# A decoder layer's opening: keys projected by token tile, the norm scale moved into the weights, bias rows built later

## The chip, the cores and the metric

One core of one Trainium2 chip. The metric is the device time of one execution in microseconds (us); less is better. The kernel before took a median of 1637.75 us in 3 runs (1637.44 to 1637.79).

## The reference, cut to what matters

```python
h = rmsnorm(x, norm_g)                       # x: 1024 tokens x 2048, float32
proj = einsum('bsd,de->bse', h, w_in)        # 5456 columns
xa, ga, q, ckv, gb, qi, ki, wi = split(proj) # ki: 64 index keys, wi: 16 head weights, ckv: 256 latent
ya = rglru(xa) * silu(ga)
yb = sparse_attention(q, rmsnorm(ckv), qi, layernorm(ki), wi, bias from rel_bias) * silu(gb)
x = x + concat(ya, yb) @ w_out
return rmsnorm(x, final_norm_g)
```

`rmsnorm(x, g)` is `x * rsqrt(mean(x*x)) * g`. The factor `g` belongs to a column of x, which is a row of `w_in`, so it can be multiplied into either.

## The kernel before, in words

Everything is float32, and each product is made of three: an operand is cut into a high part (rounded to the format that TensorE multiplies quickly) and the low rest, and `triple` adds low x high, high x low and high x high.

**Input.** x comes in 8 tiles of 128 tokens, 1 MB each (`xin`, four buffers). For a tile ScalarE (ACT) sums the squares (`square`, L704) and takes the root (`root_x`, L709). VectorE (DVE) inverts it and multiplies the tile by it and by `g_bc`, the norm scale on all partitions (`norm_x`, L1344). TensorE (PE) transposes the tile with 16 instructions (`turn_x`, L1034), ACT copies the high part out of PSUM (`high_x`, L715) and DVE makes the low part (`low_x`, L1351). The results, `hT_hi` and `hT_lo`, stay for the whole projection.

**Projection.** `w_in` is taken in 43 tiles of 128 columns (the first, `T_KW`, has the 80 columns of keys and head weights). A tile comes in four pieces, with one buffer each. SyncE (SP) issues the load when the piece's low part of the last tile is made. ACT copies the high part (`high`, L724) once PE has used the last tile's piece (`w_used`), and GpSimd (POOL) subtracts it from the raw weights (`low`, L643). PE (`project_tile`, L1023 to L1025) runs 6 matmuls of 512 columns for each of the 16 rows of blocks.

**Order on PE at the start.** The bias matmul (L1015), whose result ACT copies, 8 partitions wide, and SP stores 128 times to DRAM as `bias_rows` (1.5 MB, L459). Then the transposes. With tiles 4 to 7 goes a quarter each of the keys of the first 512 tokens; the second 512 follow. Then tile 1 (`T_C`), the means of the keys (L1070), tile 2, the variance (L1076), tile 3, the latent's mean square (L1088), and tile 4 with the index scores in it (`score`, L1110).

**Orders by hand.** Each engine runs its list in program order. On SP each load of weights stands behind the waits of all before it, and the loads of tile 1 behind the bias store. On ACT, after the keys' layer norm, stand all four pieces of `high(4)`, then an exponential with its table (L776), the latent's root (L778), and the copies of tile 3's result (`stacks`, L788 and L789), which DVE completes (L1409, L1410). The first score waits for these. Later stages (LRU from tile 11, attention projection from tile 27) run through the same `high` and `low`.

Of the kernel before, what the change touches and what calls it, by code (L numbers as in the profile page):

```python
# [117 lines left out]
def layer(nc, a, out):  # L118
# [11 lines left out]
    with ctx:  # L130
# [22 lines left out]
        w_nat = sb("w_nat", [P, QB, IH])  # L153
        sums = sb("sums", [P, QB, 3])
# [533 lines left out]
        def _(act):  # L688
# [23 lines left out]
            def high_x(i):  # L712
                for j in range(2):
                    act.wait_ge(x_tp, 2 * i + j + 1)
                    nc.scalar.activation(  # L715
                        hT_hi[:, 8 * j:8 * j + 8, i * P:(i + 1) * P],
                        x_bank(i, j).rearrange("p (t s) -> p t s", s=P), ACT.Copy).then_inc(h_hi, 1)

            def high(t, js=range(PIECES), n=P):

                for j in js:
                    act.wait_ge(w_in_s[j], 16 * t + 16)
                    act.wait_ge(w_used, 4 * t + j + 1)
                    nc.scalar.activation(w_hi[:, j, :, 0:n], w_raw[:, j, :, 0:n], ACT.Copy).then_inc(w_hi_s, 1)  # L724
# [281 lines left out]
        def _(pe):  # L1006
            nc.tensor.sem_inc(w_used, PIECES)
# [663 lines left out]
```

## Time and profile before

| | us |
|---|---|
| median of 3 runs | 1637.75 |
| the profiled execution | 1639.89 |
| its span, first to last instruction | 1638.2 |
| PE busy | 1585.0 |
| DVE busy | 855.5 |
| ACT busy | 581.0 |
| POOL busy | 424.3 |

Times on the profile's clock start at the first instruction. Matmul ends are modelled, so consecutive matmuls overlap in the rows: their pace is read from start to start. PEld is the load of a matmul's weights, which runs beside the matmul ahead of it. "Idle before" names the work that the profile holds responsible for the end of the wait.

### The profile page before, as it was taken

The numbers are of one execution on the slowest core, as the hardware profiler recorded it, in microseconds if no ns is written. First come the engines' busy times: TensorE is split into PE (matmuls) and PEld (weight loads), VectorE is DVE, ScalarE is ACT, GpSimd is POOL, SyncE is SP. The second block draws the span as 40 slices with busy tenths as digits, with TensorE's granted clock in tenths as the row PEclk, the third lists the DMA queues.
The fourth block names the chain that finished last, engine by engine and source line by source line (L and its number), as shares of the span: only waits on it lengthen the run. The fifth ranks groups of instructions, "written<-read, shape, count | busy, mean of one in ns | idle before, by whom it ended". The sixth has DMA issues, their size and how long they took to land.

```text
span 1638.2 us, 21182 instructions
## 1 busy us (share of the span) xinstructions
PE 1585.0 (97%) x7403; PEld 1314.9 (80%) x7403; DVE 855.5 (52%) x1497; ACT 581.0 (35%) x849; POOL 424.3 (26%) x285
## 2 busy tenths in 40 slices
PE   4999999999999999999999999999998899999998
PEld 3678999988888888888888888777776788888886
DVE  7417555577777877875555555277777100031003
ACT  7225555434444343332111111355555222232320
POOL 1112222222222222222222222110010344444650
PEclk8999999999999999999999999999999999999999
DMA  7411211112221122223222221321222523237322
GB/s 260 86 46 45 66 44 40 37 48 62 61 61 44 49 67 67 67 84 96 76 72 77 70 77 51 110 84 62 64 80 74 222 91 102 90 97 301 131 88 103
DMA packets 132302, 141.35 MB, mean 86 GB/s; under 512 B 8511, under 2 KB 103841, under 8 KB 129953
## 3 DMA queue, kind: packets, MB, share of 16 engines
q1 hardware_dynamic: 130720, 136.55, 26.8%
q0 software_dynamic: 1536, 4.20, 0.8%
q8 instruction: 28, 0.46, 0.1%
q14 instruction: 18, 0.14, 0.0%
HBM read 116.08 MB, written 24.64 MB: 86 GB/s over the span
## 4 chain that ended last, share of the span: by engine, by line
PE 83%; issue 8%; DVE 4%; ACT 2%; DMA 1%; DVEq 0%; POOL 0%; SPq 0%; ACTq 0%; POOLq 0%
PE ps L1023 17%; PE ps L1024 17%; PE ps L1025 17%; PE ps L1283 6%; PE ps L1285 6%; PE ps L1284 6%; PE ps L1224 2%; PE ps L1110 2%; PE ps L1112 2%; PE ps L1188 2%; PE ps L1201 1%; PE ps L1310 1%; PE ps L1309 1%; PE ps L1308 1%; PE ps L1208 1%
## 5 line engine op out<-in xcount | busy, mean ns | idle before, releaser
L1023 PE MATMUL ps<-hT_hi,w_lo 128*128 128x512 f32 (+2 forms) x1376 | 524.8, 381 | 2.5 <-POOL w_lo L643 2.5
L1024 PE MATMUL ps<-hT_lo,w_hi 128*128 128x512 f32 (+2 forms) x1376 | 522.8, 380 | 0.0
L1025 PE MATMUL ps<-hT_hi,w_hi 128*128 128x512 f32 (+2 forms) x1376 | 522.6, 380 | 0.0
L643 POOL TENSOR_TENSOR w_lo<-w_raw,w_hi 128x512 fp32r<-128x512 f32 (+1 forms) x172 | 240.5, 1402 | 780.9 <-ACT w_hi L724 780.9
L1023 PEld LDWEIGHTS ps<-hT_hi,w_lo 128*128 128x128 f32 (+1 forms) x1376 | 257.7, 187 | 49.9 <-issue 4.0
L1024 PEld LDWEIGHTS ps<-hT_lo,w_hi 128*128 128x128 f32 (+1 forms) x1376 | 257.5, 187 | 45.9 <-issue 0.4
L1025 PEld LDWEIGHTS ps<-hT_hi,w_hi 128*128 128x128 f32 (+1 forms) x1376 | 257.5, 187 | 45.6 <-issue 0.2
L724 ACT ACTIVATE w_hi<-w_raw 128x512 fp32r<-128x512 f32 (+1 forms) x172 | 106.6, 628 | 504.7 <-PE ps L1025 483.4
L1283 PE MATMUL ps<-wo_hi,hT_lo 128*128 128x512 f32 x448 | 175.2, 391 | 3.1 <-DVE hT_lo L1551 3.1
L1610 DVE TENSOR_TENSOR res<-ps,res 128x512 f32<-128x512 f32 x32 | 21.9, 691 | 295.8 <-PE ps L1285 244.9
L1284 PE MATMUL ps<-wo_lo,hT_hi 128*128 128x512 f32 x448 | 174.9, 390 | 0.0
L1285 PE MATMUL ps<-wo_hi,hT_hi 128*128 128x512 f32 x448 | 174.8, 390 | 0.0
L1459 DVE MATCH_REPLACE8 scores<-top,scores 128x384 f32<-128x384 f32 (+2 forms) x192 | 165.8, 876 | 0.0
L1454 DVE MAX8 top<-scores 128x8 f32<-128x384 f32 (+2 forms) x192 | 155.3, 879 | 0.9 <-DVE sg L1491 0.2
L679 POOL TENSOR_TENSOR wo_lo<-wo_raw,wo_hi 128x1024 fp32r<-128x1024 f32 x48 | 116.1, 2419 | 148.4 <-ACT wo_hi L956 148.4
L1434 DVE SCALAR_TENSOR_TENSOR scores<-relu,w_nat,scores 128x384 f32<-128x384 f32 (+2 forms) x96 | 94.7, 997 | 79.1 <-ACT relu L798 79.0
L956 ACT ACTIVATE wo_hi<-wo_raw 128x1024 fp32r<-128x1024 f32 x48 | 50.8, 1061 | 191.4 <-PE ps L1285 191.4
L798 ACT ACTIVATE relu<-ps 128x384 f32<-128x384 f32 (+2 forms) x96 | 72.9, 760 | 80.0 <-PE ps L1112 63.6
L1283 PEld LDWEIGHTS ps<-wo_hi,hT_lo 128*128 128x128 f32 x448 | 84.5, 189 | 20.7 <-issue 3.3
L1284 PEld LDWEIGHTS ps<-wo_lo,hT_hi 128*128 128x128 f32 x448 | 84.5, 189 | 17.7
L1285 PEld LDWEIGHTS ps<-wo_hi,hT_hi 128*128 128x128 f32 x448 | 84.5, 189 | 17.7
L1498 DVE TENSOR_TENSOR rg<-ps,ig 128x1024 f32<-128x1024 f32 x8 | 9.8, 1225 | 158.2 <-ACT ig L876 140.3
(179 smaller groups left out, 1716.8 us busy)
## 6 DMA issues: line engine op xcount, KB each, us to landing
w_raw<-in_w_in SPq DMA_DIRECT2D x168, 256.0 KB, 2.9
wo_raw<-in_w_out SPq DMA_DIRECT2D x64, 512.0 KB, 3.6
xin<-in_x SPq DMA_DIRECT2D x8, 1024.0 KB, 5.3
res<-in_x SPq DMA_DIRECT2D x8, 1024.0 KB, 9.4
out<-res SPq DMA_DIRECT2D x16, 512.0 KB, 4.0
y_lru_dram<-sg SPq DMA_DIRECT2D x8, 512.0 KB, 2.8
q_dram<-av SPq DMA_DIRECT2D x8, 512.0 KB, 3.8
gate_dram<-rg SPq DMA_DIRECT2D x8, 512.0 KB, 4.4
```

The source lines that it names most:

```text
L643: nc.gpsimd.tensor_tensor(w_lo[:, j, :, 0:n], w_raw[:, j, :, 0:n], w_hi[:, j, :, 0:n].bitcast(F32), ALU.subtract).then_inc(w_lo_s, 1)
L679: nc.gpsimd.tensor_tensor(wo_lo[:, j % 2, :, :], wo_raw[:, j % 4, :, :], wo_hi[:, j % 2, :, :].bitcast(F32), ALU.subtract).then_inc(wo_lo_ ...
L724: nc.scalar.activation(w_hi[:, j, :, 0:n], w_raw[:, j, :, 0:n], ACT.Copy).then_inc(w_hi_s, 1)
L1023: nc.tensor.matmul(o, wlo, hi, start=(kt == 0), stop=False)
L1024: nc.tensor.matmul(o, whi, lo, start=False, stop=False)
L1025: return nc.tensor.matmul(o, whi, hi, start=False, stop=(kt == KT - 1))
L1283: nc.tensor.matmul(o, hT_lo[:, kt, tok], wo_hi[:, j % 2, k, :], start=(kt == 0), stop=False)
L1284: nc.tensor.matmul(o, hT_hi[:, kt, tok], wo_lo[:, j % 2, k, :], start=False, stop=False)
L1285: last = nc.tensor.matmul(o, hT_hi[:, kt, tok], wo_hi[:, j % 2, k, :], start=False, stop=(kt == KT - 1))
L1434: stt(acc, relu[m % 2][:, 0:w], w_nat[:, q, ds(head, 1)], acc, ALU.mult, ALU.add).then_inc(ix_acc, 1)
L1454: found = step.did(nc.vector.max(top8[:, q, :], scores[:, off(q):off(q) + (q + 1) * P]))
L1459: marked = step.did(nc.vector.match_replace(left, top8[:, q, :], left, TAKEN))
```

## The change

- The scale `norm_g` comes as 16 rows, is turned into a column per block (`g_col`), and is no longer applied to x. DVE's pass over x is a `tensor_scalar`. POOL multiplies each raw weight piece by it in place, ahead of ACT's high part.
- Weights of keys are loaded behind the first two x tiles; POOL alone scales and cuts them. Each of the first four token tiles gets its keys at once, as 48 matmuls of 128 columns. With the last four goes a quarter each of tile 1 for the first 512 tokens. Keys of the second 512 and the second half of tile 1 follow.
- All transposes use the same two PSUM tiles `X`.
- The bias matmul comes after the keys, on 128 output partitions (each head 16 times). The store reads 128 partitions, and stands on SP behind the loads of tile 2. The wait for it moves to the latent's root.

```diff
--- before.py
+++ after.py
-        g_bc = s0("g_bc", [P, D])
+        kw_hi = s0("kw_hi", [P, KT, KW], F32R)
+        kw_lo = s0("kw_lo", [P, KT, KW], F32R)
...
-        bias_sb = s0("bias_sb", [NH, BR])
+        rel_wide = s0("rel_wide", [BUCKETS, NH, COPIES])
+        bias_sb = s0("bias_sb", [NH * COPIES, BR])
...
+            def x_next(i):
+                sp.wait_ge(x_tp, 2 * (i - XB) + 2)
+                sp.dma_start(xin[:, i % XB, :], x[i * P:(i + 1) * P, :]).then_inc(x_rest[i - XB], 16)
+            sp.dma_start(g_rows[:, :], a["norm_g"][0].rearrange("(k p) -> k p", p=P)).then_inc(g_in, 16)
             x_load(0)
-            sp.dma_start(g_bc[:, :], a["norm_g"].broadcast_to([P, D])).then_inc(g_in, 16)
             x_load(1)
+            weights(T_KW, COL_KI, KW)
+            for i in range(2, XB):
+                x_load(i)
+            x_next(XB)
+            x_next(XB + 1)
+            weights(T_C, COL_CKV)
+            x_next(XB + 2)
+            x_next(XB + 3)
             sp.dma_start(rel[:, :], a["rel_bias"]).then_inc(bias_in, 16)
             sp.dma_start(onehot[:, :], a["onehot"]).then_inc(bias_in, 16)
-            for i in range(2, XB):
-                x_load(i)
             sp.wait_ge(rows_clear, 1)
             rows = 0
             for name, n, m in [("conv_w", CONV * G, P), ("conv_b", G, P), ("lru_ba", G, P), ("lru_bx", G, P),
...
-            weights(T_KW, COL_KI, KW)
-            for i in range(QB - XB):
-                sp.wait_ge(x_tp, 2 * i + 2)
-                sp.dma_start(xin[:, i, :], x[(i + XB) * P:(i + XB + 1) * P, :]).then_inc(x_rest[i], 16)
+            weights(T_C + 1, COL_CKV + P)
             sp.wait_ge(bias_cp, 1)
-            sp.dma_start(bias_d.rearrange("h (p m) -> h p m", p=P),
-                         bias_sb[:, :].rearrange("h (o m) -> h o m", o=1).broadcast_to([NH, P, BR])).then_inc(bias_st, 16)
-            weights(T_C, COL_CKV)
-            weights(T_C + 1, COL_CKV + P)
+            sp.dma_start(bias_d.rearrange("h (c r m) -> (h c) r m", c=COPIES, m=BR),
+                         bias_sb[:, :].rearrange("h (o m) -> h o m", o=1).broadcast_to([P, P // COPIES, BR])
+                         ).then_inc(bias_st, 16)
             weights(T_QI, COL_QI)
             weights(T_QI + 1, COL_QI + P)
...
-            def low(t, n=P):
+            def gain(j, n):
+                return g_col[:, j * PK:(j + 1) * PK].rearrange("p (k o) -> p k o", o=1).broadcast_to([P, PK, n])
+            def scale_kw(j):
+                pool.wait_ge(w_in_s[j], 16)
+                part = w_raw[:, j, :, 0:KW]
+                nc.gpsimd.tensor_tensor(part, part, gain(j, KW), ALU.mult).then_inc(kw_g_s, 1)
+            def cut_kw(j):
+                part = slice(j * PK, (j + 1) * PK)
+                pool.wait_ge(kw_g_s, j + 1)
+                nc.gpsimd.tensor_copy(kw_hi[:, part, :], w_raw[:, j, :, 0:KW]).then_inc(w_hi_s, 1)
+                pool.wait_ge(w_hi_s, j + 1)
+                nc.gpsimd.tensor_tensor(kw_lo[:, part, :], w_raw[:, j, :, 0:KW], kw_hi[:, part, :].bitcast(F32),
+                                        ALU.subtract).then_inc(w_lo_s, 1)
+            pool.wait_ge(g_made, 1)
+            scale_kw(0)
+            for j in range(PIECES):
+                if j + 1 < PIECES:
+                    scale_kw(j + 1)
+                cut_kw(j)
+            def low(t):
                 for j in range(PIECES):
+                    part = w_raw[:, j, :, :]
+                    pool.wait_ge(w_in_s[j], 16 * t + 16)
+                    nc.gpsimd.tensor_tensor(part, part, gain(j, P), ALU.mult).then_inc(w_g_s, 1)
                     pool.wait_ge(w_hi_s, 4 * t + j + 1)
-                    nc.gpsimd.tensor_tensor(w_lo[:, j, :, 0:n], w_raw[:, j, :, 0:n],
-                                            w_hi[:, j, :, 0:n].bitcast(F32), ALU.subtract).then_inc(w_lo_s, 1)
-            low(T_KW, KW)
+                    nc.gpsimd.tensor_tensor(w_lo[:, j, :, :], part, w_hi[:, j, :, :].bitcast(F32), ALU.subtract
+                                            ).then_inc(w_lo_s, 1)
             with pool.Fori(1, TILES) as t:
                 low(t)
...
-                        x_bank(i, j).rearrange("p (t s) -> p t s", s=P), ACT.Copy).then_inc(h_hi, 1)
-            def high(t, js=range(PIECES), n=P):
+                        X[j][:, :].rearrange("p (t s) -> p t s", s=P), ACT.Copy).then_inc(h_hi, 1)
+            def high(t, js=range(PIECES)):
                 for j in js:
-                    act.wait_ge(w_in_s[j], 16 * t + 16)
+                    act.wait_ge(w_g_s, 4 * t + j - 3)
                     act.wait_ge(w_used, 4 * t + j + 1)
-                    nc.scalar.activation(w_hi[:, j, :, 0:n], w_raw[:, j, :, 0:n], ACT.Copy).then_inc(w_hi_s, 1)
+                    nc.scalar.activation(w_hi[:, j, :, :], w_raw[:, j, :, :], ACT.Copy).then_inc(w_hi_s, 1)
             act.wait_ge(eps_made, 1)
             square(0)
             root_x(0)
             square(1)
-            act.wait_ge(bias_mm, 1)
-            nc.scalar.activation(bias_sb[:, :], X[0][0:NH, 0:BR], ACT.Copy).then_inc(bias_cp, 1)
+            root_x(1)
             for i in range(QB):
-                if i + 1 < QB:
-                    root_x(i + 1)
+                high_x(i)
                 if i + 2 < QB:
                     square(i + 2)
-                high_x(i)
-                if i == XB - 2:
-                    high(0, n=KW)
-            high(1)
+                    root_x(i + 2)
+                if XB <= i:
+                    high(1, [i - XB])
             act.wait_ge(small_tp, 1)
             nc.scalar.activation(par_t[:, :], X[1][:, 0:PARS], ACT.Copy).then_inc(small_cp, 1)
-            act.wait_ge(bias_st, 16)
-            act.wait_ge(w_used, done(0))
+            act.wait_ge(bias_mm, 1)
+            nc.scalar.activation(bias_sb[:, :], X[0][:, 0:BR], ACT.Copy).then_inc(bias_cp, 1)
+            act.wait_ge(kw_used, 1)
             nc.scalar.activation(kw_sb[:, :], PJ[0][0:KW, :], ACT.Copy).then_inc(pj_free[0], 1)
             high(2)
...
             act.wait_ge(c_var, 1)
+            act.wait_ge(bias_st, 16)
...
-            pe.wait_ge(bias_in, 32)
-            nc.tensor.matmul(X[0][0:NH, 0:BR], rel[:, :], onehot[:, :], start=True, stop=True).then_inc(bias_mm, 1)
             pe.wait_ge(id_made, 1)
-            pe.wait_ge(bias_cp, 1)
-            def triple(o, j, k, tok, m):
+            pe.wait_ge(g_in, 16)
+            nc.tensor.transpose(X[0][:, 0:KT], g_rows[:, :], ident[0:KT, 0:KT]).then_inc(g_tp, 1)
+            pe.wait_ge(g_made, 1)
...
-                    pe.wait_ge(h_lo, 2 * i + j + (1 if i < XB else 3))
+                    if i > 0:
+                        pe.wait_ge(h_lo, 2 * i - 1 + j)
                     for n in range(8):
-                        last = nc.tensor.transpose(x_bank(i, j)[:, n * P:(n + 1) * P],
+                        last = nc.tensor.transpose(X[j][:, n * P:(n + 1) * P],
                                                    xin[:, i % XB, (8 * j + n) * P:(8 * j + n + 1) * P], ident[:, :])
                     last.then_inc(x_tp, 1)
-            for i in range(QB):
-                turn_x(i)
-                if i >= XB:
-                    pe.wait_ge(h_lo, 4 + 2 * XB)
-                    pe.wait_ge(w_lo_s, i - XB + 1 + PIECES)
-                    for k in range(PK):
-                        triple(PJ[0][0:KW, 0:NT], i - XB, k, slice(0, NT), KW)
-            pe.wait_ge(h_lo, 4 + 2 * QB)
-            def project_tile(t, par, turn, m=P, between=None, parts=ALL_TOKENS):
+            def keys_tokens(at, n):
+                for kt in range(KT):
+                    if kt % PK == 0:
+                        pe.wait_ge(w_lo_s, PIECES + kt // PK + 1)
+                    o, tok = PJ[0][0:KW, at:at + n], slice(at, at + n)
+                    nc.tensor.matmul(o, kw_lo[:, kt, :], hT_hi[:, kt, tok], start=(kt == 0), stop=False)
+                    nc.tensor.matmul(o, kw_hi[:, kt, :], hT_lo[:, kt, tok], start=False, stop=False)
+                    last = nc.tensor.matmul(o, kw_hi[:, kt, :], hT_hi[:, kt, tok], start=False, stop=(kt == KT - 1))
+                return last
+            def project_tile(t, par, turn, between=None, parts=ALL_TOKENS, js=range(PIECES), last_part=True):
                 pe.wait_ge(pj_free[par], turn + 1)
-                for j in range(PIECES):
+                for j in js:
                     pe.wait_ge(w_lo_s, 4 * t + j + 1 + PIECES)
                     for k in range(PK):
                         kt = j * PK + k
                         for at, tok, n in parts:
-                            last = triple(PJ[par][0:m, at:at + n], j, k, slice(tok, tok + n), m)
-                        if k == PK - 1:
+                            last = triple(PJ[par][:, at:at + n], j, k, slice(tok, tok + n))
+                        if k == PK - 1 and last_part:
                             last.then_inc(w_used, 1)
                         if between:
                             between(kt)
-            project_tile(0, 0, 0, m=KW, parts=ALL_TOKENS[1:])
+            turn_x(0)
+            for i in range(QB):
+                if i + 1 < QB:
+                    turn_x(i + 1)
+                if i < XB:
+                    pe.wait_ge(h_lo, 2 * i + 2)
+                    keys_tokens(i * P, P)
+                else:
+                    project_tile(T_C, 1, 0, parts=ALL_TOKENS[:1], js=[i - XB], last_part=False)
+            pe.wait_ge(h_lo, 2 * QB)
+            keys_tokens(NT, NT).then_inc(kw_used, 1)
             pe.wait_ge(small_in, 16 * 8)
             nc.tensor.transpose(X[1][:, 0:PARS], par_rows[:, :], ident[0:PARS, 0:PARS]).then_inc(small_tp, 1)
-            project_tile(1, 1, 0)
+            pe.wait_ge(rel_made, 1)
+            nc.tensor.matmul(X[0][:, 0:BR], rel_wide[:, :, :].rearrange("b h c -> b (h c)"), onehot[:, :],
+                             start=True, stop=True).then_inc(bias_mm, 1)
+            project_tile(T_C, 1, 0, parts=ALL_TOKENS[1:])
             pe.wait_ge(small_cp, 1)
             pe.wait_ge(pj_free[0], 2)
+            pe.wait_ge(bias_cp, 1)
...
-            dve.wait_ge(g_in, 16)
+            dve.wait_ge(g_tp, 1)
+            nc.vector.tensor_copy(g_col[:, :], X[0][:, 0:KT]).then_inc(g_made, 1)
             def norm_x(i):
                 dve.wait_ge(x_sd, i + 1)
                 root, inverse = (stat[:, k * XB + i % XB:k * XB + i % XB + 1] for k in (1, 2))
                 chain(nc.vector.reciprocal(inverse, root))
-                stt(xin[:, i % XB, :], xin[:, i % XB, :], inverse, g_bc[:, :], ALU.mult, ALU.mult
-                    ).then_inc(x_norm, 1)
+                nc.vector.tensor_scalar(xin[:, i % XB, :], xin[:, i % XB, :], inverse, None, ALU.mult
+                                        ).then_inc(x_norm, 1)
...
+            dve.wait_ge(bias_in, 32)
+            nc.vector.tensor_copy(rel_wide[:, :, :], rel[:, :].rearrange("b (h o) -> b h o", o=1).broadcast_to(
+                [BUCKETS, NH, COPIES])).then_inc(rel_made, 1)
             dve.wait_ge(x_tp, 2 * QB)
-            dve.wait_ge(bias_st, 16)
             chain(nc.vector.memset(ones_k[:, :], 1.0 / ID))
```

## Rows read from the trace of the kernel before

**Rows 1.** The page: busy time, share of the span and instructions of each engine

```profile
PE 1585.0 (97%) x7403; PEld 1314.9 (80%) x7403; DVE 855.5 (52%) x1497; ACT 581.0 (35%) x849; POOL 424.3 (26%) x285
```

**Rows 2.** Windows: length, busy us (instructions) by engine, granted clock, DMA share, GB/s

```profile
13.29:36.37 23.08, 13.62 (x81) 12.77 (x81) 21.94 (x18) 20.26 (x28) 3.40 (x4) 0.81 0.78 256
...
67.47:72.06 4.59, 4.59 (x13) 3.64 (x14) 4.55 (x7) 2.29 (x4) 3.64 (x3) 0.63 0.59 146
72.06:91.05 18.99, 18.99 (x84) 15.42 (x84) 0.54 (x4) 1.90 (x3) 3.89 (x3) 1.00 0.25 64
```

**Rows 3.** Timeline: start, us, engine, line (13.29: from the chain that ended last)

```profile
5.77 1.91 ACT L704 ACTIVATE junk<-xin 128x2048 bf16<-128x2048 f32 x1 [2.79 <-DMA xin<-in_x]
8.41 2.35 DVE L1344 SCALAR_TENSOR_TENSOR xin<-xin,stat,g_bc 128x2048 f32<-128x2048 f32 x1
10.80 1.91 ACT L704 ACTIVATE junk<-xin 128x2048 bf16<-128x2048 f32 x1 [2.69 <-DMA xin<-in_x]
...
13.29 3.66 PE ps L1034 x16
...
15.41 1.01 ACT L715 ACTIVATE hT_hi<-ps 128x1024 fp32r<-128x1024 f32 x1
16.45 1.23 DVE L1351 TENSOR_TENSOR hT_lo<-ps,hT_hi 128x1024 fp32r<-128x1024 f32 x1 [0.49 <-ACT hT_hi L715]
...
44.42 1.91 PE L1034 MATMUL ps<-ident,xin 128*128 128x128 f32 x16
```

**Rows 4.** Timeline from the bias store to the end of tile 1

```profile
29.62 0.87 SPq L459 DMA_DIRECT2D bias_rows<-bias_sb  x1
...
64.59 0.11 DVE L1363 MEMSET ones_k<- 64x64 f32 x1 [11.15 <-DMA bias_rows<-bias_sb]
...
67.47 0.47 PE L1023 MATMUL ps<-hT_hi,w_lo 128*128 128x512 f32 x1 [2.50 <-POOL w_lo L643]
...
91.05 0.64 PE L1070 MATMUL ps<-kw_sb,ones_k 64*64 64x512 f32 x1
```

**Rows 5.** Weight loads of two 128-column matmuls in a row, and mean by form

```profile
172.88 0.19 PEld L1112 LDWEIGHTS ps<-ki_hi,stack_a 128*128 128x128 f32 x1
172.99 0.19 PEld L1023 LDWEIGHTS ps<-hT_hi,w_lo 128*128 128x128 f32 x1
...
L1025 PEld LDWEIGHTS ps<-hT_hi,w_hi 128*128 128x128 f32 x1344 | 252.7, 188 | 42.8
L1025 PEld LDWEIGHTS ps<-hT_hi,w_hi 128*80 128x80 f32 x32 | 4.8, 151 | 2.8 <-issue 0.2
```

**Rows 6.** DVE and POOL groups by shape: count, busy us, mean ns

```profile
L1536 DVE TENSOR_SCALAR prob_sb<-prob_sb,sums 128x1024 f32<-128x1024 f32 x8 | 6.0, 753 | 0.3
L1536 DVE TENSOR_SCALAR prob_sb<-prob_sb,sums 128x896 f32<-128x896 f32 x8 | 5.5, 686 | 0.3
...
L643 POOL TENSOR_TENSOR w_lo<-w_raw,w_hi 128x320 fp32r<-128x320 f32 x4 | 3.4, 884 | 24.0 <-ACT w_hi L724 24.0
```

**Rows 7.** DMA from 17 to 18 us, while the keys' weights land

```profile
DMA packets 646, 0.20 MB, mean 200 GB/s; under 512 B 646, under 2 KB 646, under 8 KB 646
```

**Rows 8.** Timeline from the keys' layer norm to the first score

```profile
130.00 1.68 ACT L724 ACTIVATE w_hi<-w_raw 128x512 fp32r<-128x512 f32 x3
134.35 0.63 ACT L724 ACTIVATE w_hi<-w_raw 128x512 fp32r<-128x512 f32 x1 [2.68 <-PE ps L1025]
...
142.46 0.44 PE L1110 MATMUL ps<-ki_lo,stack_a 128*128 128x384 f32 x1 [0.61 <-DVE stack_b L1410]
```

**Rows 9.** L643 on POOL, 100 to 170 us: min/median/max ns; then its start at 130.71

```profile
L643 POOL TENSOR_TENSOR w_lo<-w_raw,w_hi x13: 1262/1296/2260, 99.5 to 169.7; 128x512 fp32r<-128x512 f32 x13
...
130.71 1.66 POOL L643 TENSOR_TENSOR w_lo<-w_raw,w_hi 128x512 fp32r<-128x512 f32 x1 [13.68 <-ACT w_hi L724]
```

**Rows 10.** Windows of tile 4 with its scores, and of one LRU group

```profile
142.46:165.00 22.54, 21.48 (x114) 19.77 (x115) 20.84 (x24) 10.34 (x16) 3.89 (x3) 1.00 0.14 49
466.00:512.24 46.24, 46.24 (x205) 38.29 (x205) 36.22 (x53) 18.44 (x22) 12.21 (x8) 1.00 0.21 60
```

More of the change, by code:

```diff
@@ L78 @@
 BR = 3 * P
+COPIES = P // NH
 OC = 512
@@ L153, in layer @@
         w_nat = sb("w_nat", [P, QB, IH])
+        g_col = sb("g_col", [P, KT])
         sums = sb("sums", [P, QB, 3])
@@ L166, in layer @@
         xin = s0("xin", [P, XB, D])
-        g_bc = s0("g_bc", [P, D])
+        kw_hi = s0("kw_hi", [P, KT, KW], F32R)
+        kw_lo = s0("kw_lo", [P, KT, KW], F32R)
         junk = s0("junk", [P, D], BF16)
         par_rows = s0("par_rows", [PARS, P])
+        g_rows = s0("g_rows", [KT, P])
         onehot = s0("onehot", [BUCKETS, BR])
         rel = s0("rel", [BUCKETS, NH])
-        bias_sb = s0("bias_sb", [NH, BR])
+        rel_wide = s0("rel_wide", [BUCKETS, NH, COPIES])
+        bias_sb = s0("bias_sb", [NH * COPIES, BR])
         p0.close()
@@ L303, in layer @@
         g_in = sem("g_in")
+        g_tp = sem("g_tp")
+        g_made = sem("g_made")
+        rel_made = sem("rel_made")
         x_in = [sem(f"x_in{i}") for i in range(XB)]
@@ L311, in layer @@
         w_in_s = [sem(f"w_in{j}") for j in range(PIECES)]
+        w_g_s = sem("w_g_s")
+        kw_g_s = sem("kw_g_s")
+        kw_used = sem("kw_used")
         w_hi_s = sem("w_hi_s")
@@ L393, in layer @@
         pool_step = sem("pool_step")
-        def x_bank(i, j):
-            return (PS[2 * (i % 2) + j] if i < XB else X[j])[:, :]
         def scored(stack, rows):
@@ L1006, in _ @@
         def _(pe):
-            nc.tensor.sem_inc(w_used, PIECES)
+            nc.tensor.sem_inc(w_used, 2 * PIECES)
             nc.tensor.sem_inc(wo_used, 2)
@@ L1012, in _, with triple @@
             nc.tensor.sem_inc(ro_mm, 4)
-            pe.wait_ge(bias_in, 32)
-            nc.tensor.matmul(X[0][0:NH, 0:BR], rel[:, :], onehot[:, :], start=True, stop=True).then_inc(bias_mm, 1)
             pe.wait_ge(id_made, 1)
-            pe.wait_ge(bias_cp, 1)
-            def triple(o, j, k, tok, m):
+            pe.wait_ge(g_in, 16)
+            nc.tensor.transpose(X[0][:, 0:KT], g_rows[:, :], ident[0:KT, 0:KT]).then_inc(g_tp, 1)
+            pe.wait_ge(g_made, 1)
+            def triple(o, j, k, tok):
                 kt = j * PK + k
                 hi, lo = hT_hi[:, kt, tok], hT_lo[:, kt, tok]
-                whi, wlo = w_hi[:, j, k, 0:m], w_lo[:, j, k, 0:m]
+                whi, wlo = w_hi[:, j, k, :], w_lo[:, j, k, :]
                 nc.tensor.matmul(o, wlo, hi, start=(kt == 0), stop=False)
@@ L1315, in _ @@
         def _(dve):
-            nc.vector.sem_inc(h_lo, 4)
             nc.vector.sem_inc(ix_acc, 8)
@@ L1350, in low_x @@
                     part = (slice(None), slice(8 * j, 8 * j + 8), slice(i * P, (i + 1) * P))
-                    tt(hT_lo[part], x_bank(i, j).rearrange("p (t s) -> p t s", s=P),
+                    tt(hT_lo[part], X[j][:, :].rearrange("p (t s) -> p t s", s=P),
                        hT_hi[part].bitcast(F32), ALU.subtract).then_inc(h_lo, 1)
```

## The prediction

> **What bounds the kernel now.** Read the page first: PE is busy 97% of the span, VectorE 52%, ScalarE 35%, GpSimd 26% [rows 1]. So only two things can move the end: PE's own work, and the 53 us in which PE stands still, with the stretches in which its clock is low. The change keeps every matmul product. Next, the windows of the opening [rows 2]. From 13.29 to 36.37 us PE works 13.62 us of 23.08, at a granted clock of 0.81, because it only transposes: x tiles are normalised one by one, and keys start with the fifth. Then the timeline [rows 4]: the bias store, issued at 29.62, holds VectorE until 64.59 us, 34 us after the end of its issue, and the loads of tile 1 crawl beside it. PE waits 2.50 us for tile 1's weights and starts at 67.47, with the clock at 0.63 up to 72.06 [rows 2]. Tile 1 ends at 91.05. I take 91.05 as the mark of the opening. Past it the order of work stays as it was, except for GpSimd's extra multiplications.
>
> A measurement of this kernel can tell about 0.2%, 3.3 us, from no change.
>
> **Part 1, the opening, step by step (new clock times).**
>
> *First tile.* The row load of the scale is issued ahead of x, about 0.4 us (an issue on this queue, the 0.87 us of the store's being the dearest [rows 4]). The first norm pass, at 8.41, lasts 2.35 us [rows 3]. It becomes a pass with one input and a factor per partition. That form takes 753 ns for 1024 elements and 686 for 896, 0.52 ns more for each element [rows 6], so 2048 take 1.29 us. PE starts transposing at 8.4 + 0.4 + 1.3 + 0.2 = 10.3, cold: 3.66 us [rows 3], to 13.9. The second x tile followed the scale's 1 MB; from 5.77 to 10.80 are 5.0 us for two MB [rows 3], so it now lands 2.5 us earlier, near 8.7. The second transposes wait for the first's copies, 1.01 on ScalarE and 1.23 on VectorE [rows 3], and end near 17.4.
>
> *Key weights.* 640 KB behind the second tile; at 200 GB/s [rows 7] 3.3 us, so from 9.6 to 12.0. GpSimd runs 12 operations: 4 scalings, 4 copies, 4 subtractions. The subtraction takes 0.884 us [rows 6]. The copy and the scaling are not in the trace: bounds 0.3 us (VectorE's rate in rows 6, with its fixed part) and 1.3 us (GpSimd's 128x512 minimum, [rows 9]); I take 0.88, the same engine and shape. 12 x 0.88 = 10.6, from 9.6 to 20.2, and 0.8 for collisions with VectorE: 21. The first tile's keys end at about 22.
>
> *Pace of a 128-column key matmul.* Two 128-column matmuls with 128-column weights have their loads 172.88 and 172.99 apart, 0.11 us [rows 5]; the weight load sets it, since 512 columns take 18.99/84 = 0.227 us [rows 2] and 128 would stream in 0.057. Loads of 80 columns are 37 ns shorter than of 128 (151 against 188, [rows 5]), so 0.11 - 0.037 = 0.07 us. Bounds 0.057 and 0.12 (a 128-column transpose: 1.91/16, [rows 3]). I take 0.07, since the shape's own load row gives it: 48 x 0.07 = 3.4 us for each token tile. The Trainium skill (TensorE: Matmul & The Clock Gate, LDWEIGHTS) gives columns/1.2 ns, thus 67 ns for 80 columns; by it the keys of a tile are 3.2 us.
>
> *Tiles 1 to 4.* Four transpositions of 1.91 and three sets of keys of 3.4 from 22: 17.8, to 39.8. ScalarE needs 2.3 us for squares and root (5.77 to 8.41, less VectorE's reciprocal of about 0.3) and two copies of 1.01 [rows 3], 4.4 us for each tile, less than PE's 5.3, so PE sets the pace; before, VectorE's pass of 2.35 and two low parts of 1.23 did [rows 3].
>
> *Tiles 5 to 7 with tile 1's first half.* A quarter is 12 x 0.227 = 2.7, with the transposition 4.6. ScalarE has its 4.4 and a high part of 0.63 [rows 8], 5.1, so it binds here: by 39.8 + 0.3 + 2.7, then twice 5.1 and a last 2.7 + 0.4 the quarters end at 55.7. Keys' second half and tile 1's second half take 48 x 0.227 = 10.9 each, parameters and bias between them 1.0 (guessed from the cold 128-column transposes, 0.23 each [rows 3]): 78.5. With 1.0 for semaphores 79.5. **Gain 11.5 us.** Bounds: 192 x (0.12 - 0.07) = 9.4 more with slow short matmuls; a cold stretch as in 67.47:72.06, where 11 matmuls went at 0.43 instead of 0.23, costs 2.2 each, none to two of them; cheap copies save 1.5. So a gain between 13 and 0.
>
> *What is moved at no cost.* The parameter rows and one-hot loads go out after the last x tile (issue near 30) and are needed near 67; 34 us cover them. The bias store starts near 68. Even at its old 35 us it ends at 103, and its new waiter, the latent's root, comes at 126. Queued behind it on SyncE are only tile 3's loads, whose buffers are not free before 74, and PE needs them at 105. Bias matmul and its ScalarE copy lie between keys and tile 1's second half, counted above.
>
> **Part 2, GpSimd's scaling of 168 pieces.** It equals the subtraction in form: 1.30 us median [rows 9]. Where pieces come 5.4 us apart, one piece needs 0.63 + 1.30 + 1.30 = 3.2 us and nothing is late. The exception is where ScalarE comes late and takes pieces in a row: at 130.00, three in 1.68 us and the fourth at 134.35 [rows 8]. `low` multiplies piece j + 1 only after it has subtracted piece j, and `high` now waits for the multiplication. So: copy to 130.6, subtraction 130.71 + 1.66 = 132.4 [rows 9]; then for the three others scaling, copy and subtraction. The first scaling meets VectorE's low part of the keys, as the old second subtraction did (2.26, [rows 9]), to 134.6; copy to 135.3; subtraction 136.7; scaling 138.0; copy 138.6; subtraction 140.0; scaling 141.3; the fourth copy starts at 141.3, not 134.35: **7.0 us late** (6.0 without the collision). Behind it on ScalarE stand exponential, root and `stacks`; behind these VectorE and the first score at 142.46, for which PE had already waited 0.61 [rows 8]. PE stands still 7.6 us in all. After 2.50 us of rest the clock fell and cost 2.2 us [rows 2]; here I take 1.5, as the stage has 1.06 us of idle PE [rows 10]. VectorE is busy 20.84 of 22.54 us there, and four scalings may block it: 0.5. **Loss 9 us**, bounds 6 and 11.
>
> In the LRU stage VectorE has 10.0 us idle in a group of 46.24 [rows 10], and eight scalings, if each blocked it fully, would take 10.4. The two-input operations that collide already (2.26 against 1.30, [rows 9]) are few, so I take nothing. The Trainium skill (SBUF — State Buffer, Who interferes with whom) says a VectorE operation with two SBUF inputs and a reading GpSimd operation block each other fully; the rows agree.
>
> **Sum.** The profiled execution's span was 1638.2 and its own time 1639.89: -11.5 + 9 = -2.5 gives 1635.7 and 1637.4. Its own time is 2.1 above the median, so the median becomes 1637.75 - 2.5 = **1635.3 us**.
>
> **Rivals.**
> *(a) The late fourth piece does not reach PE*, for instance because scalings run ahead. For it: GpSimd idles before 130. Against: its order is written out, multiply and subtract alternating. Then only the opening counts, with up to 3 us left of the loss: -8.5 to -11.5, 1627.7 for its middle. Chance 0.15.
> *(b) Slower: short matmuls run at 0.11 instead of 0.07*, in the first four tiles. Price 192 x 0.04 = 7.7: -2.5 + 7.7 = +5.2, 1643. It decides beyond 0.07 + 5.8/192 = 0.10 us. For it: the only fast-format 128-column pair in the trace is at 0.11. Against: it has wider weights. Chance 0.15.
> *(c) Slower: scalings hold VectorE through the later stages.* With 0.4 us over the slack in each of eight groups +3.2, and half of one scaling (0.65) in each of five index tiles, +3.2: -2.5 + 6.4 = +3.9, 1641.7. Chance 0.05.
> *(d) The bias store still blocks loads.* Against: tile 1's loads now precede it by 40 us; it would cost nothing seen from rows. No chance of its own.
>
> **Numbers.** Forecast 0.65, of which 0.43 within 0.2% and 0.22 beyond it on the fast side (a loss near 6, or a gain near 13). Faster 0.22 + 0.15 = 0.37, same 0.43, slower 0.15 + 0.05 = 0.20. The forecast's own range is 1631 to 1639. The range 1629 to 1642.5 leaves out half of (a) and about half of (b) and (c), less than 2 in 10.
>
> **What would show it.** Tile 1 ending near 79.5; loads of 80-column weights 0.07 us apart in the first four tiles; the fourth high part of tile 4 starting 11.3 us after the first, not 4.35; PE idle about 7.6 us before the first score with a low clock behind it; LRU groups still 46.24 us long. Wrong would be: no such idle time (then a), a mark near 87 (then b), or longer groups (then c).

## The result, and the profile after

The changed kernel takes **1661.38 us** (median; 1659.80 to 1661.87), the kernel before, run beside it, 1637.77: ratio 1.0141, 95% interval 1.0123 to 1.0159. It is 23.6 us slower where 2.5 us of gain were forecast, and outside the range. The profiled execution took 1660.93 with a span of 1659.2.

The page's busy times first (before: [rows 1]):

```profile
PE 1609.6 (97%) x7548; PEld 1320.3 (80%) x7548; DVE 848.4 (51%) x1499; ACT 580.6 (35%) x845; POOL 626.7 (38%) x461
```

PE's share is unchanged, but its busy time rose by 24.6 us, about the whole loss. So PE does not wait more: it works longer on the same products.

The opening went as predicted. Timeline of the changed kernel; columns as in [rows 3]:

```profile
8.81 1.29 DVE L1395 TENSOR_SCALAR xin<-xin,stat 128x2048 f32<-128x2048 f32 x1
...
10.24 3.65 PE L1070 MATMUL ps<-ident,xin 128*128 128x128 f32 x16 [7.25 <-DVE xin L1395]
...
18.28 0.23 PE L1082 MATMUL ps<-hT_hi,kw_hi 128*80 128x128 f32 x1
18.35 0.23 PE L1080 MATMUL ps<-hT_hi,kw_lo 128*80 128x128 f32 x1
18.42 0.23 PE L1081 MATMUL ps<-hT_lo,kw_hi 128*80 128x128 f32 x1
...
79.43 1.50 PE L1121 MATMUL ps<-kw_sb,ones_k 64*64 64x512 f32 x3
```

The norm pass takes 1.29 us, the short key matmuls start 0.07 us apart, and the mark stands at 79.43 (before 91.05, forecast 79.5).

The stall at tile 4 came too. The same view from 119 us (before: [rows 8]); L761 is the high part on ScalarE, L679 the scaling, L681 the subtraction:

```profile
119.00 0.63 ACT L761 ACTIVATE w_hi<-w_raw 128x512 fp32r<-128x512 f32 x1
123.39 0.63 ACT L761 ACTIVATE w_hi<-w_raw 128x512 fp32r<-128x512 f32 x1 [3.76 <-POOL w_raw L679]
126.39 0.63 ACT L761 ACTIVATE w_hi<-w_raw 128x512 fp32r<-128x512 f32 x1 [2.38 <-POOL w_raw L679]
129.42 0.63 ACT L761 ACTIVATE w_hi<-w_raw 128x512 fp32r<-128x512 f32 x1 [2.40 <-POOL w_raw L679]
...
121.33 2.02 POOL L679 TENSOR_TENSOR w_raw<-w_raw,g_col 128x512 f32<-128x512 f32 x1
124.09 1.27 POOL L681 TENSOR_TENSOR w_lo<-w_raw,w_hi 128x512 fp32r<-128x512 f32 x1 [0.74 <-ACT w_hi L761]
125.32 1.04 POOL L679 TENSOR_TENSOR w_raw<-w_raw,g_col 128x512 f32<-128x512 f32 x1
...
137.53 0.69 PE L1161 MATMUL ps<-ki_lo,stack_a 128*128 128x384 f32 x1 [6.28 <-DVE stack_b L1463]
```

The three late pieces wait for a scaling that stands behind a subtraction; the fourth starts 10.4 us after the first (before 4.35), and PE waits 6.28 us.

The windows of this stall, of the stretch from the mark to the first score, and of one LRU group (columns as in [rows 2]):

```profile
130.00:140.00 10.00, 3.72 (x16) 3.39 (x15) 5.87 (x18) 6.55 (x9) 4.55 (x4) 0.71 0.17 48
...
79.43:137.53 58.10, 51.82 (x241) 42.11 (x241) 17.55 (x22) 20.94 (x25) 24.01 (x21) 0.97 0.17 45
...
466.10:513.64 47.54, 47.54 (x206) 38.16 (x205) 35.95 (x53) 18.48 (x22) 21.90 (x16) 1.00 0.21 58
```

From the mark to the first score PE rests 58.10 - 51.82 = 6.28 us, which is that one wait. What no step foresaw is the last row. A group takes 47.54 us instead of 46.24 [rows 10], at the same clock of 1.00 and with no idle time on PE. Later, in the 16 attention projections, each high part waits for PE to be done with a piece (24 matmuls) and so with its buffer, so their distance is the piece's time. Timeline of ScalarE, the changed kernel and then the kernel before:

```profile
904.64 0.63 ACT L761 ACTIVATE w_hi<-w_raw 128x512 fp32r<-128x512 f32 x1 [4.97 <-PE ps L1060]
910.24 0.63 ACT L761 ACTIVATE w_hi<-w_raw 128x512 fp32r<-128x512 f32 x1 [4.05 <-PE ps L1060]
...
907.32 0.63 ACT L724 ACTIVATE w_hi<-w_raw 128x512 fp32r<-128x512 f32 x1 [4.80 <-PE ps L1025]
912.76 0.63 ACT L724 ACTIVATE w_hi<-w_raw 128x512 fp32r<-128x512 f32 x1 [4.81 <-PE ps L1025]
```

They are 5.60 us apart, and in the kernel before 5.44: each 512-column matmul starts 0.2333 us after the last instead of 0.2267, 6.7 ns or 16 cycles of 2.4 GHz more.

### The profile page after: what moved, and what is told of

Its sections match the earlier page's. It is cut to its first block, busy times and chain, and to the rows that moved or that the text cites. A ratio compares the mean times of both kernels' runs of the same rounds, so it can differ in the third digit from the quotient of the medians.

```text
span 1659.2 us, 21751 instructions
## 1 busy us (share of the span) xinstructions
PE 1609.6 (97%) x7548; PEld 1320.3 (80%) x7548; DVE 848.4 (51%) x1499; ACT 580.6 (35%) x845; POOL 626.7 (38%) x461
## 4 chain that ended last, share of the span: by engine, by line
PE 80%; issue 10%; DVE 4%; POOL 3%; ACT 2%; DMA 1%; DVEq 0%; SPq 0%; ACTq 0%; POOLq 0%
PE ps L1058 16%; PE ps L1060 16%; PE ps L1059 16%; PE ps L1335 6%; PE ps L1334 6%; PE ps L1336 6%; PE ps L1275 2%; PE ps L1161 2%; PE ps L1163 2%; PE ps L1239 2%; PE ps L1252 1%; POOL w_lo L681 1%; POOL w_raw L679 1%; PE ps L1361 1%; PE ps L1359 1%
## 5 line engine op out<-in xcount | busy, mean ns | idle before, releaser
L1058 PE MATMUL ps<-hT_hi,w_lo 128*128 128x512 f32 (+1 forms) x1344 | 518.1, 385 | 1.6 <-POOL w_lo L681 1.6
L1060 PE MATMUL ps<-hT_hi,w_hi 128*128 128x512 f32 (+1 forms) x1344 | 516.0, 384 | 0.0
L1059 PE MATMUL ps<-hT_lo,w_hi 128*128 128x512 f32 (+1 forms) x1344 | 515.9, 384 | 0.0
L681 POOL TENSOR_TENSOR w_lo<-w_raw,w_hi 128x512 fp32r<-128x512 f32 x168 | 235.6, 1402 | 581.9 <-ACT w_hi L761 581.9
L1058 PEld LDWEIGHTS ps<-hT_hi,w_lo 128*128 128x128 f32 x1344 | 252.5, 188 | 54.4 <-issue 4.1
L1059 PEld LDWEIGHTS ps<-hT_lo,w_hi 128*128 128x128 f32 x1344 | 252.4, 188 | 50.5 <-issue 0.2
L1060 PEld LDWEIGHTS ps<-hT_hi,w_hi 128*128 128x128 f32 x1344 | 252.3, 188 | 50.0
L761 ACT ACTIVATE w_hi<-w_raw 128x512 fp32r<-128x512 f32 x168 | 105.9, 631 | 503.9 <-PE ps L1060 383.9
L679 POOL TENSOR_TENSOR w_raw<-w_raw,g_col 128x512 f32<-128x512 f32 x168 | 202.4, 1205 | 8.3 <-DMA w_raw<-in_w_in 8.3
```

What stands on the lines that cost most here:

```text
L679: nc.gpsimd.tensor_tensor(part, part, gain(j, P), ALU.mult).then_inc(w_g_s, 1)
L681: nc.gpsimd.tensor_tensor(w_lo[:, j, :, :], part, w_hi[:, j, :, :].bitcast(F32), ALU.subtract).then_inc(w_lo_s, 1)
L761: nc.scalar.activation(w_hi[:, j, :, :], w_raw[:, j, :, :], ACT.Copy).then_inc(w_hi_s, 1)
L1058: nc.tensor.matmul(o, wlo, hi, start=(kt == 0), stop=False)
L1059: nc.tensor.matmul(o, whi, lo, start=False, stop=False)
L1060: return nc.tensor.matmul(o, whi, hi, start=False, stop=(kt == KT - 1))
```

## The experiments

**Theory A** came from a line of the diff that the excerpt ahead of the prediction leaves out. Tiles are allocated in the order of the code:

```diff
         sums = sb("sums", [P, QB, 3])
+        g_col = sb("g_col", [P, KT])
         sb("line_pad", [P, 8])
```

The 64 bytes a partition of `g_col` move all tiles behind them. No trace shows an address, but the built program does. In the kernel before, w_raw, w_hi and w_lo begin at bytes 149888, 158080 and 166272 of a partition, multiples of 128; now they begin 64 further on. hT_hi and hT_lo, allocated first, stay at multiples of 128. The theory: off such a multiple, the 512-byte rows of weights cost 16 cycles a matmul. (PE loads one operand, here the weights, and then streams the other, the moving one, through; here that is hT.) **Rival B**: GpSimd's scalings, 202 us of new work beside PE, slow PE's reads.

**1. g_col inside the bytes of sums**, a tile of the attention's softmax, first used when the last scaling is done:

```diff
-        g_col = sb("g_col", [P, KT])
         sums = sb("sums", [P, QB, 3])
+        g_col = sums[:, :, :].rearrange("p q k -> p (q k)")[:, 0:KT]
```

> The changed kernel with one difference: the 64 bytes a partition of g_col lie inside the tile sums instead of ahead of the weight tiles, so that w_raw, w_hi, w_lo and all that follows have the addresses of the kernel before (multiples of 128 bytes, instead of 64 above one). Theory A (the placement of the 512-byte rows of w_hi and w_lo costs 6.6 ns for each 512-column matmul): the high parts of a projection come 5.44 us apart instead of 5.60, an LRU group is back from 47.54 to about 46.24 us, the mark of the opening stays at 79.4, and the time falls from 1661.4 by the 24 us between what the marks forecast and what they show, to 1634 to 1639. Theory B (GpSimd's scalings slow the weight loads or the moving reads): nothing of that changes, 5.60 and 47.54 us, and the time stays within 3 us of 1661.

Measured: 1637.17 us, ratio to the kernel before 0.9986 (0.9976 to 0.9995). Its trace has the same scalings (202.2 us of them), but the piece is back at 5.44:

```profile
904.79 0.63 ACT L761 ACTIVATE w_hi<-w_raw 128x512 fp32r<-128x512 f32 x1 [4.81 <-PE ps L1060]
910.23 0.63 ACT L761 ACTIVATE w_hi<-w_raw 128x512 fp32r<-128x512 f32 x1 [4.81 <-PE ps L1060]
```

The groups of matmuls by form, of the changed kernel and then of this one (columns: busy us, mean ns of one):

```profile
L1058 PE MATMUL ps<-hT_hi,w_lo 128*128 128x512 f32 x1088 | 430.2, 395 | 1.6 <-POOL w_lo L681 1.6
...
L1335 PE MATMUL ps<-wo_lo,hT_hi 128*128 128x512 f32 x448 | 176.5, 394 | 0.0
...
L1058 PE MATMUL ps<-hT_hi,w_lo 128*128 128x384 f32 x256 | 87.9, 343 | 0.0
```

```profile
L1058 PE MATMUL ps<-hT_hi,w_lo 128*128 128x512 f32 x1088 | 424.1, 390 | 1.7 <-POOL w_lo L681 1.7
...
L1335 PE MATMUL ps<-wo_lo,hT_hi 128*128 128x512 f32 x448 | 174.3, 389 | 0.0
...
L1058 PE MATMUL ps<-hT_hi,w_lo 128*128 128x384 f32 x256 | 87.8, 343 | 0.0
```

In the changed kernel the 512-column forms are 5 ns longer each, the 384-column form is not. B falls: the scalings are all there. Where the 23.4 us between the two spans arise is read from the first and last start of three lines (duration ns min/median/max ahead of them), the changed kernel first:

```profile
L1189 PE MATMUL ps<-xc_hi,wg_lo x32: 388/389/395, 365.6 to 700.4; 128*128 128x512 f32 x32
L1218 PE MATMUL ps<-hT_hi,wk_lo x32: 393/394/787, 1061.2 to 1246.4; 128*128 128x512 f32 x32
L1334 PE MATMUL ps<-wo_hi,hT_lo x448: 392/392/496, 1299.9 to 1606.9; 128*128 128x512 f32 x150
```

```profile
L1189 PE MATMUL ps<-xc_hi,wg_lo x32: 389/389/389, 364.3 to 690.0; 128*128 128x512 f32 x32
L1218 PE MATMUL ps<-hT_hi,wk_lo x32: 389/391/628, 1040.6 to 1224.7; 128*128 128x512 f32 x32
L1334 PE MATMUL ps<-wo_hi,hT_lo x448: 389/389/492, 1279.5 to 1583.5; 128*128 128x512 f32 x150
```

1.3 us at the first gates, 10.4 at the last, 20.6 and 20.4 at the attention's first key and at the out projection, 23.4 at its last matmul. That is the pace: 1.3 up to the first gates, then seven groups at 1.30 (9.1), 16 attention projections of four pieces at 0.16 each (10.2), and the out projection.

**2. and 3. The kernel before, moved.** Its `line_pad` of [P, 8] is an unused tile; here it is [P, 24] and [P, 16].

> The kernel before with 64 bytes a partition more in line_pad, so that w_raw, w_hi, w_lo and what follows lie 64 bytes further on; nothing is computed otherwise and GpSimd does no scaling. Theory A: high parts 5.60 us apart instead of 5.44, an LRU group 47.5 us instead of 46.24, the time 1637.8 + 168 pieces of 0.16 = 1664.7 at most, about 1661. Theory B: 1637.8, unchanged.

> The kernel before with 32 bytes a partition more in line_pad: the weight tiles lie 32 above a multiple of 128. If any place off a multiple of 128 costs the same (a row of 512 bytes then touches a fifth block of 128): 5.60 us for a piece and about 1661 us. If only 64 is dear: 1638. If the price grows with more, finer misalignment: over 5.60 us. Theory B: 1637.8.

Measured: 1664.68 us for 64 bytes (ratio 1.0150, 1.0122 to 1.0179), 1665.94 in a single run for 32. Both have 5.60 us for a piece. Nothing of the change is in these kernels, so the placement alone makes the loss. The two differ in the out projection, where PE loads hT and `wo` is the moving operand; see 5.

**4. Which tile's place counts.** First 64 bytes between w_raw and w_hi. The tiles of the attention (`s3`) and of the out projection (`s4`), which use the same bytes later, are moved by 64 too:

```diff
         w_raw = sbp("w_raw", [P, PIECES, PK, P])
+        sbp("raw_pad", [P, 16])
         w_hi = sbp("w_hi", [P, PIECES, PK, P], F32R)
...
         s3 = alloc(ph)
+        s3("pad3", [P, 16])
...
         s4 = alloc(ph)
+        s4("pad4", [P, 16])
```

> The kernel before with 64 bytes a partition between w_raw and w_hi: w_raw keeps its address, w_hi and w_lo (the weights that PE loads) and the work tiles behind them lie 64 bytes further on; hT (the moving operand) is where it was. If the place of the loaded weights sets the pace: pieces 5.60 us apart, about 1661 us, as with everything moved. If the place of w_raw does (ScalarE and GpSimd read it, the loads write it): 5.44 us and 1638.

Measured, in a single run: 1662.43 us. With w_raw at its old place:

```profile
902.85 0.63 ACT L727 ACTIVATE w_hi<-w_raw 128x512 fp32r<-128x512 f32 x1 [4.97 <-PE ps L1028]
908.45 0.63 ACT L727 ACTIVATE w_hi<-w_raw 128x512 fp32r<-128x512 f32 x1 [4.97 <-PE ps L1028]
```

So the place of w_raw, which the transfers write and ScalarE and GpSimd read, is not what costs. This experiment alone does not tell PE's loads from the writes of w_hi and w_lo by ScalarE and GpSimd, whose place moved as well; 5 does, with hT, which PE alone touches in the projections. Moving w_lo without w_hi was not tried.

**5. The moving operand.** The 32 bytes of `line_pad` ahead of hT_hi instead of behind sums, so that the weights stay home; the small tiles between hT and the weights move along:

```diff
+        sb("pad0", [P, 8])
         hT_hi = sb("hT_hi", [P, KT, S], F32R)
...
-        sb("line_pad", [P, 8])
```

> The kernel before with the 32 bytes of line_pad placed ahead of hT_hi instead of behind: all weight tiles keep their addresses, hT_hi, hT_lo (the moving operand of the projections, the loaded one of the out projection) and ident lie 32 bytes further on. If only the loaded operand's place counts: pieces 5.44 us apart, an LRU group 46.24, and the out projection's 512-column matmuls at 0.233 us, +9 us, 1646. If either operand's place counts: both at 0.233, about 1664. If neither (the price comes of two weight tiles against each other): 1638.

Measured, in a single run: 1668.14 us, and in the projections:

```profile
901.91 0.63 ACT L724 ACTIVATE w_hi<-w_raw 128x512 fp32r<-128x512 f32 x1 [4.97 <-PE ps L1025]
907.51 0.64 ACT L724 ACTIVATE w_hi<-w_raw 128x512 fp32r<-128x512 f32 x1 [4.97 <-PE ps L1025]
```

The theory was too narrow: the moving operand off its place costs the 16 cycles too. To see how far off, one more move of all weight tiles, `line_pad` of [P, 32]:

> The kernel before with 96 bytes a partition more in line_pad. If any place off a multiple of 128 bytes costs the same for the loaded weights: pieces 5.60 us apart and 1661 to 1666 us. In the out projection, where wo is the moving operand, 64 bytes gave 0.2289 us a matmul and 32 bytes 0.2333: 96 shows whether 64 is the exception (0.2333 again) or the price falls with the distance (under 0.2289).

Measured, in a single run: 1671.33 us; 5.62 us for a piece. Start to start of some 140 out-projection matmuls from 1399.8 us (first and last start, by their count), and the piece in the projections:

| kernel | piece, us | out projection: moved | us a matmul |
|---|---|---|---|
| before, and 1 | 5.44 | nothing | 0.2267 |
| changed; 2; 4 (by 64) | 5.60 | moving, 64 | 0.2289 |
| 3 (weights by 32) | 5.60 | moving, 32 | 0.2333 |
| weights by 96 | 5.62 | moving, 96 | 0.2333 |
| 5 (hT by 32) | 5.60 | loaded, 32 | 0.2333 |

With the other operand at home, every move of the loaded one costs the full price. Of the moving one 32 and 96 do, and 64 about a third (2.2 ns).

What these rows can't tell, because each of them moves one operand alone, two other stretches of the same traces do: **when both operands are moved by the same bytes, nothing is lost.** In experiment 5 the last chunk of the out projection keeps its weights in hT (L1308), so that both operands are 32 bytes off. And in the changed kernel both operands of the gate matmuls (L1189: wg and xc) are 64 off, between projections (L1058) where only the loaded one is. Every third matmul, experiment 5 first:

```profile
1613.39 0.40 PE L1283 MATMUL ps<-wo_hi,hT_lo 128*128 128x512 f32 x1
1614.09 0.40 PE L1283 MATMUL ps<-wo_hi,hT_lo 128*128 128x512 f32 x1
...
1629.77 0.39 PE L1308 MATMUL ps<-hT_hi,hT_lo 128*128 128x512 f32 x1
1630.45 0.39 PE L1308 MATMUL ps<-hT_hi,hT_lo 128*128 128x512 f32 x1
```

```profile
414.51 0.39 PE L1189 MATMUL ps<-xc_hi,wg_lo 128*128 128x512 f32 x1
415.19 0.39 PE L1189 MATMUL ps<-xc_hi,wg_lo 128*128 128x512 f32 x1
...
415.87 0.39 PE L1058 MATMUL ps<-hT_hi,w_lo 128*128 128x512 f32 x1
416.57 0.39 PE L1058 MATMUL ps<-hT_hi,w_lo 128*128 128x512 f32 x1
```

Three matmuls take 0.70 us with one operand off, and 0.68, as in the kernel before, with both off alike (over the whole last chunk 42.9 us for 189 starts, before 42.8). The gates reach this pace after their first five or six matmuls. So what costs is that the two operands lie differently against multiples of 128 bytes, not that one lies off them. GpSimd is busy 1.86 of the gates' 2.80 us, with a subtraction and a scaling of moved tiles, and the price is gone all the same: a contention with it is not what costs either.

The Trainium skill (SBUF — State Buffer, Specifications (TRN2)) gives 16-byte lines, each with full bandwidth once at least two accesses fall into it, and no wider unit. By that alone, contiguous rows moved by 32, 64 or 96 bytes would cost nothing; the runs disagree (5.60 us against 5.44), and the measurement decides.

**6. The stall of tile 4.** As kernel 1, with GpSimd's loop split, so that the scalings no longer stand behind subtractions:

```diff
                 for j in range(PIECES):
                     part = w_raw[:, j, :, :]
                     pool.wait_ge(w_in_s[j], 16 * t + 16)
                     nc.gpsimd.tensor_tensor(part, part, gain(j, P), ALU.mult).then_inc(w_g_s, 1)
+                for j in range(PIECES):
+                    part = w_raw[:, j, :, :]
                     pool.wait_ge(w_hi_s, 4 * t + j + 1)
```

> As the first kernel of this series, and GpSimd multiplies all four pieces of a tile before it subtracts the first low part. Under theory A with the stall of tile 4 as the prediction has it (the fourth high part waits for scalings that stand behind subtractions): the high parts of tile 4 come as close as before (4.4 us from first to fourth instead of 10.4), the first score comes 5 to 6 us earlier than in the first kernel, and the time is 5 to 7 us below it, about 1630. If the stall has another cause (VectorE late, the loads of tile 4): as the first kernel, within 1.5 us. Under theory B about 1655.

Measured: 1629.78 us, ratio to the kernel before 0.9941 (0.9919 to 0.9962), 7.4 below kernel 1. From its timeline:

```profile
117.40 1.68 ACT L763 ACTIVATE w_hi<-w_raw 128x512 fp32r<-128x512 f32 x3
121.75 0.63 ACT L763 ACTIVATE w_hi<-w_raw 128x512 fp32r<-128x512 f32 x1 [2.68 <-PE ps L1062]
...
124.41 3.04 POOL L679 TENSOR_TENSOR w_raw<-w_raw,sums 128x512 f32<-128x512 f32 x3
...
124.75 0.72 DVE L1449 TENSOR_TENSOR sp_t<-sp_t 128x8 f32<-128x8 f32 x1
125.50 0.97 DVE L1450 TENSOR_TENSOR sp_t<-sp_t 128x8 f32<-128x8 f32 x1
...
131.08 0.96 DVE L1465 TENSOR_TENSOR stack_b<-ps,stack_b 64x768 fp32r<-64x768 f32 x1
...
132.09 0.44 PE L1163 MATMUL ps<-ki_lo,stack_a 128*128 128x384 f32 x1 [2.84 <-DVE stack_b L1465]
```

The first and fourth high parts are 4.35 us apart again. The first score comes 4.6 us earlier than in kernel 1 (136.69), not 5 to 6, because PE still waits 2.84 us, now for VectorE. Of the 4.6, 0.8 is there at the mark already (78.46 against 79.23), and that is scatter: kernel 6, profiled once more beside kernel 8, has its mark at 79.34. By the first gates the lead is 6.7 us (357.6 against 364.3); the granted clock, 0.89 instead of 0.77 between 130 and 145 us, is a part of this. The last 1.0 arises in the attention and is not explained.

**7. No scalings at all** in tiles 1 to 42. This is kernel 1 with the norm's scale left out of these tiles, so it computes something else and gives a price only:

```diff
-                    pool.wait_ge(w_in_s[j], 16 * t + 16)
-                    nc.gpsimd.tensor_tensor(part, part, gain(j, P), ALU.mult).then_inc(w_g_s, 1)
...
-                    act.wait_ge(w_g_s, 4 * t + j - 3)
+                    act.wait_ge(w_in_s[j], 16 * t + 16)
```

> The first kernel of this series (g_col inside sums) without GpSimd's multiplications for weight tiles 1 to 42: the norm's scale is left out of these tiles, ScalarE takes each piece as soon as its load has landed. Beside the first kernel (1637.2) this gives the price of all scalings. If the stall of tile 4 is all they cost: as the kernel with the scalings ahead, 1629.8, within 1.5 us. If they also hold VectorE or delay pieces in later stages: 1626 or less.

Measured: 1627.72 us (ratio 0.9930, 0.9904 to 0.9956): all scalings together cost kernel 1 9.5 us, and 2.1 of them are left with the scalings ahead, a little more than the 1.5 allowed. (Kernels 1 and 6 ran on another chip; the kernel before took 1639.53 beside this one and 1639.04 beside those.) Its timeline shows the same small operation without a scaling beside it:

```profile
124.95 0.17 DVE L1446 TENSOR_TENSOR sp_t<-sp_t 128x8 f32<-128x8 f32 x1
...
129.87 0.44 PE L1159 MATMUL ps<-ki_lo,stack_a 128*128 128x384 f32 x1 [0.61 <-DVE stack_b L1461]
```

It takes 0.17 us against 0.97 (L1450 above) for an operation on 8 elements: VectorE is held for about the length of a scaling (1.04). The Trainium skill (SBUF — State Buffer, Who interferes with whom) says that a VectorE operation with two SBUF inputs and a reading GpSimd operation exclude each other; here the trace agrees. It is not only these: the operation behind L1450, with one input (L1451), took 0.97 us too.

**8. A version that uses this**: kernel 6 with the 14 small operations on the decay parameters, needed only at the LRU stage, moved on VectorE behind the last index tile's stack subtractions.

```diff
-            dve.wait_ge(sp_exp, 1)
...
             stacks(T_QI + 7, 0)
+            dve.wait_ge(sp_exp, 1)
...
             add_scores(T_QI + 7)
```

The lines left out are the 14 operations, as they were.

> The kernel with the scalings ahead, and VectorE's 13 small operations on the decay parameters (sp_t) moved from before tile 4's two stack subtractions to behind those of the last index tile, where VectorE waits 2.6 us. Theory: what is left between the kernel with the scalings ahead (1629.8) and the one without scalings (1627.7) is that GpSimd's scalings of tile 5 stretch three of the small operations from 0.17 to 0.72 and 0.97 us while the stack subtractions, for which PE waits 2.84 us, stand behind them. Then PE's wait falls to about 0.6 us, the first score comes 2.2 us earlier, and the time is 1627.6. Rival: the scalings stretch the stack subtractions themselves by as much, or the moved operations delay the last index tile: 1629.8, unchanged.

> The kernel with the scalings ahead once more, on the same chip as the one with the decay parameters later, as its yardstick: 1629.8 us, within 1.5.

Measured: 1627.74 us (1626.98 to 1629.88), ratio to the kernel before 0.9929 (0.9917 to 0.9941); kernel 6 beside it 1630.72 (1629.09 to 1631.32), so 3.0 less where 2.2 were reckoned. The wait is down to 0.61 us, and the first score comes 2.2 us earlier, as reckoned:

```profile
129.85 0.44 PE L1163 MATMUL ps<-ki_lo,stack_a 128*128 128x384 f32 x1 [0.61 <-DVE stack_b L1452]
```

This is 10.9 us faster than the kernel before beside it, and 33.6 less than the change as it was made took on another chip. It recovers what kernel 7 gains by leaving the scalings out.

## Why the prediction was wrong

**The step that failed** is the one sentence under which all matmuls past tile 1 were costed at nothing: "Past it the order of work stays as it was, except for GpSimd's extra multiplications." The order did stay; the addresses did not, and the loaded weights came to lie otherwise than hT. "LRU groups still 46.24 us long" was the check, and it read 47.54. The missing term is 1.3 up to the first gates + 7 x 1.30 + 16 x 0.64 + 2.9 (1344 out-projection matmuls at 2.2 ns) = 23.5 us; the spans of the changed kernel and kernel 1 differ by 23.4. No rival held it: (c), which also had longer groups, had VectorE as the cause, and in the 47.54 us VectorE is busy only 35.95. Nothing in the trace of before shows an address. The code did: an unused tile `line_pad` of 32 bytes just ahead of the weights has no other purpose than where they begin.

**Part 1 was right.** Mark 79.43 against 79.5, and 78.4 to 79.3 in the traces of kernels 1, 6, 7 and 8; short matmuls 0.07 as taken, so rival (b) fell. Some of its terms met by luck: GpSimd's 12 operations on the keys' weights took 10.5 us (9.48 to 19.96), where 10.6 and 0.8 were reckoned, but a copy took 0.45 and a scaling 0.72 instead of 0.88, and others that ran beside VectorE's work (a copy of 1.46, a subtraction of 1.72) made up for it. Three numbers in its working are off without weight: the quarters' sum as written gives 56.1, not 55.7 (the keys behind them start at 56.00); 192 x (0.12 - 0.07) is 9.6; and the cold stretch of the kernel before holds 9 matmuls at 0.43, so 1.8 us, not 11 and 2.2.

**Part 2 was right in its mechanism, a little high in its size.** The delay of the fourth piece was reckoned with 1.30 us for a scaling, the subtraction's time; it takes 1.04 when alone, so the fourth piece came 10.4 us after the first, not 11.3, and PE's wait was 6.28 instead of 7.6. In all, 9 us were forecast as the price of the scalings, and kernel 7 gives back 9.5. Kernel 6 shows that the order of scaling and subtracting makes this stall, and that rival (a) would have been real: "for instance because scalings run ahead" gives 1629.8 where 1627.7 was reckoned.

**The sum of these two parts**, read where the addresses are as before, is kernel 1: span 1635.8 against a forecast of 1635.7, time 1637.17 beside 1639.04, 1.9 us less where 2.5 were forecast. That the loss by later scalings was "nothing" held but for 2 us at tile 4 itself: 0.5 had been put there for VectorE, and kernels 7 and 8 show some 2.2.

**Rival (d)**, a bias store that blocks loads, cost nothing, as said: the window from 79.43 to 137.53 has no idle time of PE beyond the 6.28.

## What to carry to other kernels

In a kernel that PE bounds, the place of its operand tiles is part of the work: before costing untouched matmuls at nothing, add up the bytes of every new tile allocated ahead of them, see whether the loaded and the moving operand still lie alike against multiples of 128 bytes, and look for pads. Put a small new tile behind the large ones, or into a tile that is idle then. A multiplication given to an idle engine should run ahead of that engine's waiting instructions, and the other engine's small two-input operations should not stand between it and PE.

## What the hardware showed that was not expected

- A 512-column matmul starts every 0.2267 us when the rows of both operands begin at multiples of 128 bytes, or both 32 or both 64 bytes off; every 0.2333 when only the loaded operand is 32 or 64 bytes off, or only the moving one 32 or 96; 384-column matmuls, 343 and 343 ns, don't notice. Why 16 cycles, and why 64 bytes cost the moving operand only a third, stays open.
- The weight loads' own durations don't show it: L1060 loads for 252.3 us in 1344 instructions, before 252.7 [rows 5]. The price stands in the matmuls' start-to-start times, and in part (5 of the 6.7 ns) in their durations.
